# Two layers of a hybrid mixer: projection chunks, gates and group norms in another order

## What is computed

```
h = rmsnorm(x, g_pre) @ w_in
(a_q, a_k, a_v, b_b, b_c, b_x, c_q, c_kv, c_kr, d_q, d_k, d_v, gate) = split(h)
ya = swa_sink_attention(a_q, a_k, a_v, sinks)          # 4 heads, window 128
yb = b_b * (conv3(b_c * b_x) + conv_b)                 # gated convolution over tokens, 256 channels
yc = mla(c_q, c_kv, c_kr, ...)                         # latent attention, 4 heads
yd = stick_breaking_attention(d_q, d_k, d_v)           # 4 heads
y = rmsnorm(stack([ya, yb, yc, yd]), g_grp)            # each group of 256 channels by itself
y = y * silu(gate)                                     # gate: 1024 channels
x = x + rmsnorm(y @ w_out, g_post)
```

## Time and profile before

| | us |
|---|---|
| median of 3 runs | 1676.64 |
| lowest, highest | 1673.36, 1678.78 |
| profiled execution | 1680.26 |
| its span, first to last instruction | 1678.4 |
| second layer's mixer in it | from 216.7 to 410.4 |

### The profile page before, as it was taken

How to read it: one execution, slowest core, us unless ns; L and a number is a source line. 1 busy time by engine, 2 the same in 40 slices (tenths; PEclk the granted TensorE clock), 3 DMA queues, 4 the chain that set the end, 5 groups by cost and what they waited for, 6 DMA issues and landing times.

```text
span 1678.4 us, 18593 instructions
## 1 busy us (share of the span) xinstructions
PE 1497.7 (89%) x7260; PEld 934.8 (56%) x7260; DVE 599.2 (36%) x1239; ACT 467.9 (28%) x1030; POOL 30.8 (2%) x34
## 2 busy tenths in 40 slices
PE   4998789977979979779999997979989879999996
PEld 4777367753768867344444332768867344443432
DVE  2233223342585564321211114486473331121113
ACT  2253122621551234202212111452234202121211
POOL 0000000000011000000000000002000000000000
PEclk9999899988989999869999998889999969999998
DMA  7332052232220232409989872221132409889870
GB/s 304 104 123 99 29 202 101 101 100 104 101 76 26 76 106 99 172 11 391 374 367 410 357 320 104 76 76 51 52 125 79 174 25 372 349 365 414 355 323 25
DMA packets 43722, 298.64 MB, mean 178 GB/s; under 512 B 5088, under 2 KB 5600, under 8 KB 10224
## 3 DMA queue, kind: packets, MB, share of 16 engines
q1 hardware_dynamic: 41920, 287.46, 43.9%
q10 hardware_dynamic: 1712, 9.94, 1.6%
HBM read 296.33 MB, written 1.05 MB: 177 GB/s over the span
## 4 chain that ended last, share of the span: by engine, by line
PE 78%; DVE 13%; ACT 5%; issue 2%; DMA 1%; POOLq 0%; DVEq 0%; ACTq 0%
PE ps L847 22%; PE ps L1401 14%; PE ps L1429 7%; PE ps L1444 4%; PE ps L864 3%; PE ps L1469 3%; PE ps L1027 3%; PE ps L1305 3%; PE ps L1226 1%; PE ps L1217 1%; PE ps L1231 1%; PE ps L1500 1%; PE ps L997 1%; DMA few_all<-few 1%; DVE res L2272 1%
## 5 line engine op out<-in xcount | busy, mean ns | idle before, releaser
L847 PE MATMUL ps<-hT,ring 128*128 128x272 f32 (+1 forms) x2016 | 495.6, 402 | 3.9 <-DVE hT L1937 2.7
L847 PEld LDWEIGHTS ps<-hT,ring 128*128 128x128 f32 x2016 | 390.9, 198 | 86.4 <-issue 12.1
L1401 PE MATMUL ps<-ring,arena 128*64 128x512 f32 x672 | 190.2, 600 | 0.0
L2421 DVE TENSOR_TENSOR arena<-arena,ps 128x256 f32<-128x256 f32 x32 | 13.5, 421 | 294.6 <-ACT arena L1872 294.6
L1401 PE MATMUL ps<-projT,arena 128*64 128x512 f32 x352 | 116.6, 598 | 1.1 <-DVE arena L2422 1.1
L1401 PEld LDWEIGHTS ps<-ring,arena 128*64 128x64 f32 x672 | 54.3, 137 | 88.4 <-issue 88.3
L1429 PE MATMUL ps<-ring,arena 128*64 128x512 f32 x336 | 79.4, 592 | 0.0
L1444 PEld LDWEIGHTS ps<-arena 128*128 128x128 f32 x512 | 62.8, 200 | 26.5 <-issue 24.3
L1646 ACT ACTIVATE projT<-ps 128x272 f32<-128x272 f32 x68 | 27.0, 398 | 177.5 <-PE ps L847 176.0
L1444 PE MATMUL ps<-arena 128*128 128x128 f32 x512 | 69.1, 291 | 2.0 <-DVE arena L2405 2.0
L1856 ACT ACTIVATE arena<-ps 128x512 f32<-128x512 f32 x64 | 38.2, 597 | 106.9 <-PE ps L1444 106.7
(11 more groups left out here) (422 smaller groups left out, 1777.8 us busy)
## 6 DMA issues: line engine op xcount, KB each, us to landing
ring<-experts SPq DMA_DIRECT2D x126, 1024.0 KB, 9.4
projT<-experts SPq DMA_DIRECT2D x66, 1024.0 KB, 9.0
ring<-w_in SPq DMA_DIRECT2D x64, 1024.0 KB, 4.9
ring<-w_out SPq DMA_DIRECT2D x16, 1024.0 KB, 5.0
prm<-params ACTq DMA_DIRECT2D x2, 2048.0 KB, 7.9
cst<-consts ACTq DMA_DIRECT2D x1, 2688.0 KB, 9.8
prm<-params ACTq DMA_DIRECT2D x2, 1152.0 KB, 9.3
res<-x SPq DMA_DIRECT2D x1, 1024.0 KB, 7.5
```

Source lines behind the costliest of these rows:

```text
L847: mm = pe.matmul(ps[:, 5 + j % banks, 0:ncols], w[:, j % 2, k, :], hT[:, k, T - ncols:T], start=(k == 0), stop=(k == KC - 1))
L1401: mm = pe.matmul(ps[64 * e:64 * e + 64, 0, :], xg[:, 4 * h + k, 64 * e:64 * e + 64], w[e][:, 512 * k:512 * k + 512], start=(h == 0 and k = ...
```

## The change

The columns of the convolution (CB, CC, CX) are projected ahead of the gates instead of behind them. Chunks go to two PSUM banks (5 and 6) instead of three; bank 7, now free, takes all four group sums, which lay in banks 4 and 3. The steps stand at other chunks: the scores of jobs 2 and 3 one and two chunks earlier, norm 0 behind turn 2, the stick steps earlier, the convolution behind chunks 21 and 22, norm 3 behind chunk 27. The third group is now the convolution and the fourth the stick one (`GROUP_ORDER`). The product with the gate leaves the norm step; a new step, "finish" i, does it for both chunks of a group in one DVE instruction once their gates are there. The gates are projected in the groups' order. The output projection uses banks 0 and 1 for the first half of the tokens and 5 and 6 for the second, and waits for the last chunk's copy only ahead of the second half. Some scratch tiles (`l1`, `ysq`, `yrs`) move to other places in the scratch memory.

```diff
--- before.py
+++ after.py
@@ -37,7 +37,7 @@
 SLOT = 2048
 
 
-MQ, MKV, MKR, SV, DV, SQ, SK, DQ, DK, GATE, CB, CC, CX = 0, 2, 3, 4, 5, 7, 9, 11, 13, 15, 23, 25, 27
+MQ, MKV, MKR, SV, DV, SQ, SK, DQ, DK, CB, CC, CX, GATE = 0, 2, 3, 4, 5, 7, 9, 11, 13, 15, 17, 19, 21
 N1 = 29
 ITEMS_P1 = (N1 + 1) // 2
 ITEMS_WO = 4
@@ -74,18 +74,18 @@
 
 
 
-GROUP_ORDER = [2, 0, 3, 1]
+GROUP_ORDER = [2, 0, 1, 3]
 
 
 def mixer_order_1():
 
 
     after = {3: [("latent_sums",)], 5: [("latent_q",)], 6: [("latent_k",)], 7: [("latent_v",)], 8: [("latent_rot",)],
-             9: [("tokens",)], 10: [("scores", 0)], 11: [("scores", 1)], 12: [("turn", 0)], 13: [("weigh", 0)],
-             14: [("scores", 2)], 15: [("turn", 1)], 16: [("weigh", 1)], 17: [("scores", 3)], 18: [("turn", 2)],
-             19: [("weigh", 2)], 20: [("turn", 3)], 21: [("weigh", 3)], 22: [("stick_z",)], 23: [("stick_soft",)],
-             24: [("norm", 0)], 25: [("stick_sums",)], 26: [("stick_probs",), ("norm", 1)],
-             27: [("stick_out",), ("conv", 0)], 28: [("norm", 2), ("conv", 1), ("norm", 3)]}
+             9: [("tokens",)], 10: [("scores", 0)], 11: [("scores", 1)], 12: [("turn", 0)], 13: [("weigh", 0), ("scores", 2)],
+             14: [("turn", 1)], 15: [("weigh", 1), ("scores", 3)], 16: [("turn", 2), ("norm", 0)], 17: [("weigh", 2)],
+             18: [("turn", 3)], 19: [("weigh", 3)], 20: [("stick_z",)], 21: [("stick_soft",), ("conv", 0)],
+             22: [("norm", 1), ("conv", 1)], 23: [("stick_sums",), ("norm", 2)],
+             25: [("stick_probs",)], 26: [("stick_out",)], 27: [("norm", 3)]}
     order = []
     for j in range(N1):
         order.append(("project", j))
@@ -93,7 +93,10 @@
             order.append(("sigmoid", j - GATE))
         if 1 <= j - GATE < KC + 1:
             order.append(("gate", j - GATE - 1))
+            if (j - GATE) % 2 == 0:
+                order.append(("finish", (j - GATE) // 2 - 1))
         order += after.get(j, [])
+    order += [("gate", KC - 1), ("finish", 3)]
     return order
 
 
@@ -530,12 +533,11 @@
 
         sp1 = projT[:, 0:4, 0:SEQ]
         sp2 = projT[:, SV:SV + 2, :].rearrange("p a b -> p (a b)")[:, 0:512].rearrange("p (a b) -> p a b", a=4)
-        l1 = projT[:, SQ:SQ + 4, 0:SEQ]
+        l1 = sg[:, 4:8, :]
         l2 = projT[:, DQ:DQ + 2, :].rearrange("p a b -> p (a b)")[:, 0:512].rearrange("p (a b) -> p a b", a=4)
 
-        ysq = [s1.rearrange("p a h n -> p (a h n)")[:, 512 * i:512 * i + 512].rearrange("p (c n) -> p c n", c=2)
-               for i in range(4)]
-        yrs = [pT1.rearrange("p a n -> p (a n)")[:, SEQ * i:SEQ * i + SEQ] for i in range(4)]
+        ysq = [x[:, 2 * i:2 * i + 2, :] for x in (qh, kh) for i in range(2)]
+        yrs = [vC.rearrange("p a n -> p (a n)")[:, SEQ * i:SEQ * i + SEQ] for i in range(4)]
 
 
         cv, a2 = more(0, 12, T)
@@ -852,6 +854,8 @@
 
                 for t in banks:
                     c0 = COL[t] - META
+                    if t == 2:
+                        pe.wait_ge(s("projection_copied"), N1)
                     for i, pair in enumerate(chunk_pairs):
                         if t == min(banks):
                             w = item_in(pe, (1, l, first_item + i))
@@ -881,7 +885,7 @@
                 for step in mixer_order_1():
                     kind = step[0]
                     if kind == "project":
-                        project_chunk(1, l, step[1], SEQ, 3)
+                        project_chunk(1, l, step[1], SEQ, 2)
                     elif kind == "latent_sums":
 
                         pe.wait_ge(s("latent_squares"), 1)
@@ -963,8 +967,6 @@
                         mm.then_inc(s("stick_sums_done"), 1)
                     elif kind == "stick_out":
                         pe.wait_ge(s("stick_probs_ready"), 1)
-
-                        pe.wait_ge(s("group_rms_ready"), 2)
                         for h in range(4):
                             o = ps[64 * (h % 2):64 * (h % 2) + 64, 4, SEQ * (h // 2):SEQ * (h // 2 + 1)]
                             pe.matmul(o[:, 0:SEQ], vD[:, 0, 64 * h:64 * h + 64], sp1[:, place(h), :], start=True, stop=False)
@@ -980,11 +982,10 @@
 
                             pe.wait_ge(s("group_rms_ready"), i)
                         for c in range(2):
-                            mm = pe.matmul(ps[:, 4 - i // 2, SEQ * (i % 2):SEQ * (i % 2 + 1)], ones, ysq[i][:, c, :],
+                            mm = pe.matmul(ps[:, 7, SEQ * (i % 2):SEQ * (i % 2 + 1)], ones, ysq[i][:, c, :],
                                            start=(c == 0), stop=(c == 1))
                         mm.then_inc(s("group_sums_done"), 1)
-                pe.wait_ge(s("projection_copied"), N1)
-                project_out(l, {1: 5, 2: 0}, yT, ITEMS_P1, GROUP_ORDER, s("group_ready"))
+                project_out(l, {1: 0, 2: 5}, yT, ITEMS_P1, GROUP_ORDER, s("group_ready"))
                 new_layer(pe, l + 1)
 
 
@@ -1558,7 +1559,7 @@
                         a.wait_ge(s("projected"), j + 1)
                         if j % 2 == 1 or j == N1 - 1:
                             a.sem_inc(ring_used, 1)
-                        L(a.activation(projT[:, j, META:T], ps[:, 5 + j % 3, 0:SEQ], ACT.Copy), s("projection_copied"))
+                        L(a.activation(projT[:, j, META:T], ps[:, 5 + j % 2, 0:SEQ], ACT.Copy), s("projection_copied"))
                         if j == MKV:
                             L(a.activation(sq3, projT[:, MQ:MQ + 3, META:T], ACT.Square), s("latent_squares"))
                     elif kind == "latent_sums":
@@ -1608,10 +1609,10 @@
                             a.wait_ge(s("conv_ready"), 1)
                         L(a.activation(ysq[i], yT[:, c:c + 2, :], ACT.Square), s("group_squares"))
                         a.wait_ge(s("group_sums_done"), i + 1)
-                        rsqrt_act(a, L, yrs[i], ps[:, 4 - i // 2, SEQ * (i % 2):SEQ * (i % 2 + 1)], 1.0 / 256, eps6, s("group_rms_ready"))
+                        rsqrt_act(a, L, yrs[i], ps[:, 7, SEQ * (i % 2):SEQ * (i % 2 + 1)], 1.0 / 256, eps6, s("group_rms_ready"))
                 for t in (1, 2):
                     a.wait_ge(s("out_projected"), t)
-                    b = 5 if t == 1 else 0
+                    b = 0 if t == 1 else 5
                     L(a.activation(xn[:, t - 1, :], ps[:, b:b + 2, :].rearrange("p a b -> p (a b)"), ACT.Square,
                                    accum_out=ssum[:, t:t + 1]))
                     rsqrt_act(a, L, rstd[:, t:t + 1], ssum[:, t:t + 1], 1.0 / D, eps6, s("out_rms_ready"))
@@ -2018,12 +2019,16 @@
                         for c in range(2 * GROUP_ORDER[i], 2 * GROUP_ORDER[i] + 2):
                             V(v.scalar_tensor_tensor(out=yT[:, c, :], in0=yT[:, c, :], scalar=prm1("g_grp")[:, c:c + 1],
                                                      in1=yrs[i], op0=ALU.mult, op1=ALU.mult))
-                            V(v.tensor_tensor(yT[:, c, :], yT[:, c, :], sg[:, c, :], ALU.mult),
-                              s("group_ready") if c % 2 else None)
+                    elif kind == "finish":
+
+                        i = step[1]
+                        c = 2 * GROUP_ORDER[i]
+                        V(v.tensor_tensor(yT[:, c:c + 2, :], yT[:, c:c + 2, :], sg[:, 2 * i:2 * i + 2, :], ALU.mult),
+                          s("group_ready"))
                 v.wait_ge(s("params_late"), 16)
                 for t in (1, 2):
                     v.wait_ge(s("out_rms_ready"), t)
-                    b = 5 if t == 1 else 0
+                    b = 0 if t == 1 else 5
                     o = ps[:, b:b + 2, :].rearrange("p a b -> p (a b)")
                     V(v.scalar_tensor_tensor(out=xn[:, t - 1, :], in0=o, scalar=rstd[:, t:t + 1], in1=prm1("g_post"),
                                              op0=ALU.mult, op1=ALU.mult))
@@ -2505,8 +2510,9 @@
  ...
     kv0, kv1 = r[1][:64], r[1][64:]
+    gates = [r[12][256 * i:256 * i + 256] for i in GROUP_ORDER]
     cols1 = np.concatenate([r[6], r[7], np.tile(r[8], 4), r[2], r[11], r[0], kv0, kv0, kv1, kv1, r[9], r[10],
-                            r[12], r[3], r[4], r[5], np.tile(r[8], 4)])
+                            r[3], r[4], r[5], *gates, np.tile(r[8], 4)])
     a2 = np.cumsum([0, 512, 512, 512, 512, 4, 4, 512, 512, 512, 512, 64, 8])
     q = [np.arange(a2[i], a2[i + 1]) for i in range(12)]
     heads = [q[i][P * c:P * (c + 1)] for c in range(HEAD_PAIRS) for i in (6, 7, 8)]
```

## The result

| | before | changed |
|---|---|---|
| median of 4 runs | 1676.88 | 1694.74 |
| lowest, highest | 1673.36, 1678.78 | 1688.80, 1695.48 |
| profiled execution | 1680.26 | 1688.80 |
| its span | 1678.4 | 1687.0 |
| second block begins at | 411.20 | 423.47 |

The ratio of the changed kernel's time to that of before is 1.0099, with a 95% interval of 1.0081 to 1.0117: it is slower, by some 17 us (the two medians differ by 17.9). The profiled execution is the quickest of the changed kernel's four. Since the change lies in the first mixer alone, the fifth row is the one to compare: there the changed kernel is 12.3 us behind. The last row is the rest of the span, and it differs although its instructions are the same.

The account below looks back on a forecast made before the run. It took TensorE, busy for 89% of the span, as the bound, standing still before the first mixer's norm sums. Waits +7.1 and clock +3.2 us made +10.3 over the median of 1676.64: 1686.9 us, range 1680 to 1694.

Parts of the forecast that it names:

- Direction and cause: First mixer: slower, as TensorE waits longer before the norm sums for Squares queued on ScalarE; +10.3 us in all.
- The waits: TensorE before turn 2 and the four norm sums: 18.14 us a layer against 14.57, +7.1 us in both layers.
- turn 2 and norm 0: Behind chunk 16, after the scores of job 3: together wait 4.20 us a layer, however it splits.
- norms 1, 2 and 3: Norm sums behind chunk 22, the stick sums and chunk 27: waits of 5.18, 5.95 and 2.81 us a layer.
- The last wait: Before norm 3 at the mixer's end: 6.38 us becomes 2.81, and the output projection starts without a wait.
- Two banks at no cost: Projection chunks: chunk 23's possible 1.2 us wait for a copy hides under norm 1's longer wait, so nothing.
- The clock: Low TensorE clock behind the norm waits: 5.9 us a layer against 4.3, +3.2 us in both layers.
- the first rival: Every long norm wait costs clock in full, giving the upper end, 1692 us; chance 0.16.
- my halves: Clock lost behind norms 0 and 3: half of 1.7 us, 0.85 us each.
- The second block at no difference: After the first mixer: the change touches nothing else, so no term beyond run-to-run differences of some 2 us.

Follow-up runs that it names:

- norm1_early: The changed kernel with norm 1 alone moved from behind chunk 22 to behind weigh 3 (chunk 19); median 1679.90 us, 1.0028 of before.
- after_filled: The changed kernel with 5, 10, 12 and 5 extra matmuls, results overwritten, in the waits before the four group sums; median 1675.67 us, 0.9998 of before.
- norm2_late: The changed kernel with norm 2 alone moved from behind the stick sums to behind chunk 25; median 1680.42 us, 1.0032 of before.
- before_shifted: The kernel before with 14 extra matmuls ahead of the first chunk of each first-mixer layer; median 1687.40 us, 1.0066 of before.

## Why the prediction was right, and where it was short

*Direction and cause* held: slower, by the waits before the norm sums. *The waits*: printed values are 2.75, 4.99, 5.78, 2.65 and 0.73 for turn 2; with 0.16 us each that is 17.7 against 18.14 worked out. The 0.4 us are missing at turn 2 and norm 0 (3.8 instead of 4.20); norms 1, 2 and 3 came to within 0.05. In printed values the difference to before is 16.2 + 1.3 - 12.3 - 1.7 = 3.5 us a layer, 7.0 in both, against 7.1. Each of the three moved norms, one by one, gave back the wait that its chain explains. *The last wait* of 6.4 us went, and the output projection started at full clock.

*Two banks at no cost* was right, and for the reason given, that norm 1's wait hides it: norm1_early shows the 1.0 us as soon as that wait is gone. The advice of the Trainium skill ("Perfetto Trace Analysis", Optimizing Tensor Performance), that independent groups should rotate through different banks, is seen there and not in the changed kernel.

*The clock* was the step that failed in size: "for norms 0 and 3, between none and 1.7, half of it", and 2.1 each for norms 1 and 2, 5.9 us a layer. Measured are 8.2. All four waits cost clock, norms 0 and 3 their full 1.5 and 1.7. That was the first rival, given 0.16. So the change in clock was 3.9 us in the second layer instead of 1.6, and 4.3 in the first (8.5 against 4.2, windows of 1 us). With 3.5 us of waits in each that makes +15.2; the mixer's end moved by +12.3 us (5.35 and 6.92 by layer), of which the quicker start of the changed kernel's profile hides 1.7, against +10.3 forecast. The other 1.2 us between these sums are not accounted for. That the profile came within 2 us of the sum is thus in part luck. after_filled confirms the size: without these losses the mixer is 15.2 us shorter. The rule of the Trainium skill ("TensorE: Matmul & The Clock Gate", HAM oscillation), that every long enough pause is paid anew, fits this kernel better than my halves: all four waits of the changed kernel paid, those of 2.65 and 2.75 us too. It does not settle every case, since norm2_late's wait of 2.68 us paid nothing.

*The second block at no difference* is the other miss, which the prediction did not price beyond "run-to-run differences of some 2 us". Between +12.3 us and the median's +17.9 lie 5.6 us. The profiled executions are unlike their medians in opposite directions (before 3.4 above, changed 5.9 below), and the second profile, with a second block 6.7 us longer, is near the changed kernel's median. Some 3.9 us, or 5.6 less the 1.7 of the start, are thus left for the second block, where the two profiles of the changed kernel differ by more than that (6.7). The median of 1694.74 is just over the range's end of 1694; over all ten runs of the changed kernel it is 1693.5.

What stays open is what decides the clock of the second block. If its start does, then by less than the 0.3 us between 423.47 and 423.73, which gave 1263.5 and 1270.2 us; 419.54 in before_shifted gave 1267.3. Why it should be longer more often in the changed kernel isn't shown.

## What to carry to other kernels

A step on a strictly ordered engine costs not what it takes but what stands ahead of its input on the other engine's queue: before moving a matmul up, write out the other queue from the last common point, and put the step where that queue has just run dry (here ahead of the logarithms, not behind them). Price each wait of TensorE twice, once as the wait and once as the clock behind it; here the second was half of the first (8.2 us beside 16.2 in the second layer of the changed kernel). And judge a change by the profile's stage that it touches, since stages behind it can move by several us by themselves.

## What the runs showed of the hardware

Waits of 2.65 to 2.75 us cost 1.5 to 1.7 us of clock each in the changed kernel, while in before a wait of 2.12 (printed) cost nothing and one of 2.74 cost 1.7; norm2_late has one of 2.68 us whose group sum took 1.13 us, at full clock. So a wait's length alone doesn't settle it at this size. Filling the waits with matmuls whose results are thrown away held the granted clock at 1.00 over 90 us and won 15.2 us without shortening any chain. Two profiles of the same program differed by 6.7 us in the second block, with PE equally busy (25.25 of 26 us) and the clock at 0.92 and 0.78 in the stretch shown. The same first four chunks took 14.1 us in some executions and 15.5 to 15.8 in others, with the granted clock put at 1.00 in both.
